# High matmuls of a piece first, the second mixer's projection as 512-column matmuls with folds, its tanh one slot later

## What is computed

```python
h = x
for i in range(2):
    u = rmsnorm(h, norm_mix_g[i])
    h = h + (rglru_mixer if i == 0 else ssd_mixer)(u, ...)
    h = h + swiglu(rmsnorm(h, norm_ffn_g[i]), w_gate[i], w_up[i], w_down[i])
    h = h + sigmoid(rmsnorm(h, norm_ple_g[i]) @ ple_w_gate[i]) * (p[i] @ ple_w_proj[i])
return rmsnorm(h, final_norm_g)

def ssd_mixer(u, ...):
    z, xbc, dt = split(u @ w_in)                  # 4096, 6144 and 64 columns
    xbc = silu(causal_dwconv(xbc, conv_w, conv_b))    # four taps
    xs, B, C = split(xbc)                         # 64 heads of 64; 8 groups of 128 states
    y = ssd_scan(xs, softplus(dt + dt_bias), -exp(a_log), B, C) + d_skip * xs
    y = y * silu(z)
    y = group_rmsnorm(y) * norm_g                 # 8 groups of 512
    return y @ w_out
```

## Time and profile before

| | us |
|---|---|
| median of three runs | 2766.11 |
| the three runs | 2753.71, 2766.11, 2769.26 |
| the profiled execution | 2769.57 |
| its span, first to last instruction | 2767.8 |
| mean granted TensorE clock | 0.993 |
| PE busy | 2708.5 |
| DVE busy | 2031.0 |
| ACT busy | 1342.2 |
| POOL busy | 382.6 |

### The profile page before, as it was taken

How to read it: one execution, slowest core, us unless ns; L and a number is a source line. 1 busy time by engine, 2 the same in 40 slices (tenths; PEclk the granted TensorE clock), 3 DMA queues, 4 the chain that set the end, 5 groups by cost and what they waited for, 6 DMA issues and landing times.

```text
span 2767.8 us, 51496 instructions
## 1 busy us (share of the span) xinstructions
PE 2708.5 (98%) x17871; PEld 2464.4 (89%) x17871; DVE 2031.0 (73%) x2802; ACT 1342.2 (48%) x1818; POOL 382.6 (14%) x418
## 2 busy tenths in 40 slices
PE   7999999999999999999999999999999999999997
PEld 7998888888888888999998999988888888888897
DVE  8887876665666677888886788878666556666776
ACT  5665344444444444456664566634444444444443
POOL 3333200000000121201110011121000000001122
PEclk9999999999999999999999999999999999999999
DMA  5555566656656665555555655556555666565554
GB/s 194 185 180 157 177 197 189 190 175 191 203 190 189 191 191 163 188 169 178 173 178 167 198 172 173 179 157 197 182 186 179 178 201 185 187 187 171 184 178 149
DMA packets 158369, 502.35 MB, mean 181 GB/s; under 512 B 17792, under 2 KB 20160, under 8 KB 157120
## 3 DMA queue, kind: packets, MB, share of 16 engines
q1 hardware_dynamic: 158192, 501.04, 58.1%
q10 hardware_dynamic: 80, 0.07, 0.0%
HBM read 498.88 MB, written 2.16 MB: 181 GB/s over the span
## 4 chain that ended last, share of the span: by engine, by line
PE 83%; DVE 9%; issue 4%; ACT 3%; POOL 1%; DMA 0%; DVEq 0%; ACTq 0%; SPq 0%; POOLq 0%
PE bank L381 42%; PE bank L383 21%; PE bank L364 6%; PE bank L366 6%; PE bank L365 6%; DVE wlo L821 3%; DVE arena L973 2%; ACT whi L575 1%; DVE R L878 0%; DVE arena L975 0%; PE bank L540 0%; DVE arena L1201 0%; PE bank L544 0%; ACT arena L755 0%; PE bank L542 0%
## 5 line engine op out<-in xcount | busy, mean ns | idle before, releaser
L381 PE MATMUL bank<-R,whi 128*128 128x512 f32 x4992 | 1754.5, 397 | 12.0 <-POOL R L1323 6.1
L821 DVE TENSOR_TENSOR wlo<-wraw,whi 128x1024 fp32r<-128x1024 f32 (+3 forms) x1056 | 1208.4, 1155 | 575.6 <-ACT whi L575 572.7
L575 ACT ACTIVATE whi<-wraw 128x1024 fp32r<-128x1024 f32 (+3 forms) x1056 | 993.2, 947 | 955.8 <-PE bank L383 767.1
L383 PE MATMUL bank<-R,wlo 128*128 128x256 f32 x4992 | 1395.2, 279 | 0.0
L381 PEld LDWEIGHTS bank<-R,whi 128*128 128x128 f32 x4992 | 939.5, 188 | 240.3 <-POOL R L1323 8.4
L383 PEld LDWEIGHTS bank<-R,wlo 128*128 128x128 f32 x4992 | 943.2, 189 | 0.1
L364 PE MATMUL bank<-R,whi 128*128 128x256 f32 x2368 | 683.6, 289 | 21.6 <-DVE R L878 13.0
L365 PE MATMUL bank<-R,whi 128*128 128x256 f32 x2368 | 673.0, 284 | 0.0
L366 PE MATMUL bank<-R,wlo 128*128 128x256 f32 x2368 | 672.9, 284 | 0.0
L364 PEld LDWEIGHTS bank<-R,whi 128*128 128x128 f32 x2368 | 456.7, 193 | 30.2 <-issue 15.5
L365 PEld LDWEIGHTS bank<-R,whi 128*128 128x128 f32 x2368 | 457.6, 193 | 2.2 <-issue 1.9
(11 more groups left out here) (165 smaller groups left out, 1365.7 us busy)
## 6 DMA issues: line engine op xcount, KB each, us to landing
wraw<-in_F SPq DMA_DIRECT2D x352, 512.0 KB, 3.9
wraw<-in_B SPq DMA_DIRECT2D x224, 512.0 KB, 3.6
wraw<-in_A SPq DMA_DIRECT2D x96, 512.0 KB, 3.8
wraw<-in_F SPq DMA_DIRECT2D x128, 384.0 KB, 3.1
wraw<-in_F SPq DMA_DIRECT2D x128, 320.0 KB, 3.2
wraw<-in_PL SPq DMA_DIRECT2D x64, 320.0 KB, 3.2
wraw<-in_PL SPq DMA_DIRECT2D x64, 256.0 KB, 2.8
arena<-cs_rows SPq DMA_DIRECT2D x8, 1024.0 KB, 5.8
```

The lines of the kernel that those rows point to most:

```text
L381: nc.tensor.matmul(dst.rearrange("p (s t) -> p s t", s=2), whi[:, q % RING, cols], src[:, :, k, :], start=first, stop=False)
L383: mm = nc.tensor.matmul(dst[:, 0:SEQ], wlo[:, q % RING, cols], src[:, 0, k, :], start=False, stop=last)
L575: nc.scalar.activation(whi[:, slot, 0:w * BLOCK], wraw[:, slot, 0:w * BLOCK], ACT.Copy).then_inc(w_hi, 1)
L821: V.tensor_tensor(wlo[:, slot, 0:w * BLOCK], wraw[:, slot, 0:w * BLOCK], whi[:, slot, 0:w * BLOCK].bitcast(F32), ALU.subtract).then_inc(w_ ...
```

## The change

1. `piece` waits for the high half of the weights, issues the high matmuls of all blocks of the piece, then waits for the low half and issues the low matmuls of all blocks. This holds for every stage, with two high matmuls per block in the narrow ones.
2. B1 joins `WIDE`: its high product becomes one matmul of 512 columns. DVE evacuates with `fold` and a multiply in SBUF.
3. In B1 the tanh of tile nt on ACT and its silu on DVE move from the odd step 2 nt + 3 to the even step 2 nt + 4, behind the taps of the next tile; for the sixth tile they stay at step 13, and the silu goes ahead of the wait for PE.

```diff
--- before.py
+++ after.py
@@ -48,7 +48,7 @@
 LAST_HEAD = {0: (0, 1, 2), 1: (3, 4), 2: (5, 6), 3: (7,)}
 
 
-WIDE = ("A2", "F1", "F2", "B2")
+WIDE = ("A2", "F1", "F2", "B1", "B2")
 GELU_C = 0.7978845608028654
 GELU_S = 0.044715 ** 0.5
 
@@ -368,18 +368,20 @@
             def piece(ph, it, q, blocks):
 
                 p = it * len(ph["widths"]) + ph["piece0"] + q
-                pe.wait_ge(w_lo, p + 1)
+                pe.wait_ge(w_hi, p + 1)
                 for b, (before, dst, src, k, first, last) in enumerate(blocks):
                     for s, v in before:
                         pe.wait_ge(s, v)
                     cols = slice(b * BLOCK, (b + 1) * BLOCK)
-                    if ph["name"] not in WIDE:
-                        mm = three(dst[:, 0:SEQ], whi[:, q % RING, cols], wlo[:, q % RING, cols], src[:, 0, k, :],
-                                   src[:, 1, k, :], first, last)
-                        continue
-
-                    nc.tensor.matmul(dst.rearrange("p (s t) -> p s t", s=2), whi[:, q % RING, cols], src[:, :, k, :],
-                                     start=first, stop=False)
+                    if ph["name"] in WIDE:
+                        nc.tensor.matmul(dst.rearrange("p (s t) -> p s t", s=2), whi[:, q % RING, cols], src[:, :, k, :],
+                                         start=first, stop=False)
+                    else:
+                        nc.tensor.matmul(dst[:, 0:SEQ], whi[:, q % RING, cols], src[:, 0, k, :], start=first, stop=False)
+                        nc.tensor.matmul(dst[:, 0:SEQ], whi[:, q % RING, cols], src[:, 1, k, :], start=False, stop=False)
+                pe.wait_ge(w_lo, p + 1)
+                for b, (before, dst, src, k, first, last) in enumerate(blocks):
+                    cols = slice(b * BLOCK, (b + 1) * BLOCK)
                     mm = nc.tensor.matmul(dst[:, 0:SEQ], wlo[:, q % RING, cols], src[:, 0, k, :], start=False, stop=last)
                 mm.then_inc(w_used, 1)
 
@@ -743,10 +745,6 @@
                                 group_rinv(group - 1)
                             if q == 8 and not first:
                                 group_hi(group - 1, it - 1)
-                            if q % 2 == 1 and 3 <= q <= 13:
-                                nt = q // 2 - 1
-                                act.wait_ge(conv_done, group * 6 + nt + 1)
-                                nc.scalar.activation(cth[:, nt % 2, :], ca[:, nt, :], ACT.Tanh).then_inc(conv_t, 1)
                             if q % 2 == 0 and 2 <= q <= 12:
                                 nt = q // 2 - 1
                                 if nt == 0 and not very_first:
@@ -756,6 +754,10 @@
                                                      bias=flat(bpar[:, at(group), nt * 5 + 4:nt * 5 + 5]),
                                                      scale=flat(bpar[:, at(group), nt * 5 + 3:nt * 5 + 4])
                                                      ).then_inc(tap_done, 1)
+                            if q % 2 == 0 and 4 <= q <= 12 or q == 13:
+                                nt = (q + 1) // 2 - 2
+                                act.wait_ge(conv_done, group * 6 + nt + 1)
+                                nc.scalar.activation(cth[:, nt % 2, :], ca[:, nt, :], ACT.Tanh).then_inc(conv_t, 1)
                             if q == 2 and not first:
                                 y_square(group - 1)
                             if q in (14, 16, 18):
@@ -1125,22 +1127,25 @@
                                 later_taps(cpad[:, nt % 2], ca[:, nt, :],
                                            lambda k, nt=nt, group=group: flat(bpar[:, at(group), nt * 5 + k:nt * 5 + k + 1]),
                                            conv_done)
-                            if q % 2 == 1:
-                                dve.wait_ge(w_used, p + 1)
-                                src = bank[BANKS2[q // 2 % 2]][:, 0:SEQ]
-                            if q % 2 == 1 and q < 12:
-                                nt = q // 2
-                                V.tensor_tensor(cpad[:, nt % 2, 3:3 + SEQ], src, rinv[:], ALU.mult).then_inc(bank_free, 1)
-                            if q % 2 == 1 and 3 <= q <= 13:
-                                nt = q // 2 - 1
+                            if q % 2 == 0 and 4 <= q <= 12 or q == 13:
+                                nt = (q + 1) // 2 - 2
                                 dve.wait_ge(conv_t, group * 6 + nt + 1)
                                 V.scalar_tensor_tensor(out=ca[:, nt, :], in0=cth[:, nt % 2, :], scalar=1.0,
                                                        in1=ca[:, nt, :], op0=ALU.add, op1=ALU.mult).then_inc(silu_done, 1)
+                            if q % 2 == 1:
+                                dve.wait_ge(w_used, p + 1)
+                                src = BANKS2[q // 2 % 2]
+                            if q % 2 == 1 and q < 12:
+                                nt = q // 2
+                                row = cpad[:, nt % 2, 3:3 + SEQ]
+                                fold(src, row)
+                                V.tensor_tensor(row, row, rinv[:], ALU.mult).then_inc(bank_free, 1)
                             if q % 2 == 1 and q > 12:
                                 j = q // 2 - 6
                                 if j == 0 and not very_first:
                                     dve.wait_ge(yn_lo, group * 4)
-                                V.tensor_tensor(zt[:, j, :], src, rinvh[:], ALU.mult).then_inc(bank_free, 1)
+                                fold(src, zt[:, j, :])
+                                V.tensor_tensor(zt[:, j, :], zt[:, j, :], rinvh[:], ALU.mult).then_inc(bank_free, 1)
                             if q in (14, 16, 18):
                                 z_silu(group, q // 2 - 7)
                             if q == 14:
@@ -1201,7 +1206,7 @@
                         V.scalar_tensor_tensor(out=zt[:, j, :], in0=zt[:, j, :], scalar=flat(bpar[:, at(group), 34 + j:35 + j]),
                                                in1=grms[:], op0=ALU.mult, op1=ALU.mult).then_inc(yn_done, 1)
 
-                steps(dve, ph, body, own, {"A1": 18, "B1": 21, "F1": 6, "PL": 0}.get(name, 4))
+                steps(dve, ph, body, own, {"A1": 18, "B1": 31, "F1": 6, "PL": 0}.get(name, 4))
                 own.close()
             dve.wait_ge(h_done, 2 * KT)
             V.tensor_tensor(swi_u[:, 0, :], h[:, KT - 1, :], h[:, KT - 1, :], ALU.mult).then_inc(last_square, 1)
```

## The result

The changed kernel takes 2782.23 us (median of five runs, 2781.48 to 2783.18). The kernel before, run beside it, takes 2766.11 (five runs, 2753.71 to 2771.18). The ratio is 1.0074, 95% interval 1.004 to 1.0108: slower by 0.7%. The forecast was 2758. All five runs of the changed kernel lie within 1.7 us, those of the kernel before within 17.5. The profiled execution took 2781.48 us, with a span of 2779.7 and a mean granted clock of 0.988.

The account below looks back on a forecast made before the run. PE, busy 98% of the span, was taken as the bound, so time is its issue intervals plus few gaps. 2769.6 - 15.3 (rate) - 4.8 (low-half waits) + 5.1 (operand waits) + 3.4 (B1) = 2758 us; range 2732 to 2786.

Parts of the forecast that it names:

- (a): Wide stages, high first: 226.7 + 120 = 346.7 ns a block, no alternation left for the long rhythm; -15.3 us.
- long rhythm: Wide stages: slower rate of alternating matmuls, 353.2 against 346.5 ns a block, costing 15.3 us; rival that it stays, 2773, chance 0.15.
- (c): A1, A2, B2: after a late operand of the last block, eight low matmuls are still to come; +5.1 us.
- fixed cost of 13.3 ns per matmul: Wide and narrow matmuls: one fixed cost each, whatever the order, explains both forms and gives 346.7 ns a block.
- a 512 costs its 0.231 behind another too: Rival, wide stages: 351 ns a block, +7.2 us instead of -15.3, total 2781; chance 0.14.
- The rival in which the weight loads vanish: Wide stages: loads hidden behind 512 columns, 333 ns a block, 81 us less instead of 15.3, total 2692; chance 0.10.
- (d): B1 in wide form: PE 17.0 us less, DVE 7.2 us more a group; B1 in all +3.4 us.
- (e): B1, tanh one slot later: clears the ring in which ACT waited for DVE's taps and DVE for the next whi.
- 46.9 - 4.0: B1, DVE's path to the sixth silu: 46.9 us less 4.0 idle, plus seven folds, gives 47.9 to 48.2 us.
- B1 not bound by DVE: Rival, B1: folds hide in the waits for PE, groups of 62.3 us, total 2732; chance 0.12.
- (b): PL and B1's start: waiting for low halves after the high matmuls wins -4.8 us, clock effects included.
- Clearly slower: Whole kernel: slower than 2779.9 us; chance 0.15.

Follow-up runs that it names:

- the mixture in pairs: The changed kernel with high-first order in batches of two blocks (two high matmuls, then two low); 2772.47 us in one run.
- the late product: The changed kernel with POOL's 1024-wide product in B1 waiting for the sixth silu instead of the second; 2769.66 us, ratio 1.0031.
- The last experiment: Narrow B1, old order in wide stages, high first in B1 and PL, late tanh and product, plus PL's gate bank emptied before the low half; 2754.54 us, ratio 0.9945.
- old order with late product: Kernel before with narrow B1, high first only in B1 and PL, tanh one slot later, POOL's product after the sixth silu; 2752.69 us, ratio 0.9963.

## Why the prediction was wrong, point by point

The profiled execution took 2781.5 us where the sum was 2758. Four terms account for 23 of these 23.5 us. The largest, and the one that turned a gain into a loss, is the rate of the wide form: -15.3 us were set down for it, and about -1 came.

**(a) The rate of the wide form: the mechanism right in part, the term mis-sized.** The step "227 + 120 = 346.7 ns a block everywhere" failed. The long rhythm did go, and one rate took the place of two. But it is 349.2 to 350.3, as each row of wide matmuls starts with intervals of 228 to 236 behind the narrow ones. The wide stages, A2 and B2 among them, changed by +0.5 us (table) where -15.3 for the rhythm and +4.3 for the operand waits had been set down, -11.0 together: 11.5 us off. The rate is more than that. The 4992 wide blocks x 2.7 ns (349.4 on average less 346.7) are 13.5 us, and by the stages the rate gave -0.8 instead of -15.3, 14.5 us off: +6.5 and -7.4 in F1 and F2, -1.2 in A2 (256 blocks, 353.8 to 349.1 ns), +1.3 in B2 (512 blocks, 346.6 to 349.1). The operand waits of A2 and B2 gave 3.0 of it back, see (c).

The reasoning from a fixed cost of 13.3 ns per matmul fitted the two forms of before by coincidence: the earlier trace rows had the alternation 231 and 115, and the mixture in pairs shows 233 and 114 to 119. The rival "a 512 costs its 0.231 behind another too" (2781) is nearest in time, and its even point of 348 ns was passed. Its clear loss was to begin at 351, and 349 to 350 is a little below that; so it holds for five of the eight intervals. The rest of the loss came from B1 and the other terms, and the agreement of its number with the result is luck. The rival in which the weight loads vanish is excluded: 230 ns on average, where the rule of the Trainium skill quoted in the prediction ("TensorE: Matmul & The Clock Gate") gives 216. Why the first five intervals of a row are longer stays open.

**(d), (e) B1: engine right, size wrong by 6.4 us.** DVE bounds the wide B1, as forecast; the late product shows it. The path to the sixth silu came to 48.6 (forecast 47.9 to 48.2), and from PE's start behind it to the end of piece 19 took 18.4 (1311.26 to 1329.65), as forecast. But the group is 67.2, and not 66.3. The step "46.9 - 4.0" plus seven folds failed, by 0.7. It took all waits for a whi or a tap off, and 0.37 of them stayed; with the two other idle times of the row (0.18 and 0.56 before, 0.18 and 0.47 now) that is 0.3. The rest is busy time: POOL's product was in the 46.9 already, where it stretched an operation by 1.55 us, and it stretches another by 2.04 now. The other 0.2 are from the silu's end to PE's start (1311.07 to 1311.26). The sum left this step out; it took 0.14 before (1364.89 to 1365.03). The wait was also not where it was expected. PE did not wait for the silu; it waited 2.8 us from start to start at piece 12, and the clock fell behind that. This used up what PE had to spare, but lengthened the group by under 0.1 us.

The last group of a half is shorter on the same path, 1396.92 to 1444.65, 47.7 us. Its taps show where:

```profile
1396.92 0.69 DVE L965 TENSOR_REDUCE arena<-bank 128x256 f32<-128x512 f32 x1 [0.47 <-PE bank L385]
...
1406.73 1.00 DVE L975 SCALAR_TENSOR_TENSOR arena<-arena,bpar 128x256 f32<-128x256 f32 x2
1407.77 1.41 DVE L977 SCALAR_TENSOR_TENSOR arena<-arena,bpar 128x256 f32<-128x256 f32 x1
...
1444.23 0.42 DVE L1133 SCALAR_TENSOR_TENSOR arena<-arena 128x256 f32<-128x256 f32 x1
```

From the first tap to the last are 1.04 us, where the groups before take 1.25 (1272.21 to 1273.46, above). Over six tiles the difference is 1.3 us, of which 0.4 go again elsewhere on the path. What makes the taps closer is not shown; the kernel before has it too. The steady groups cost 4 x 1.34 + 2 x 1.1 = 7.6 us (forecast 3.9), the first group of half 0 +3.8 (forecast +1.6; 1.1 of it by the order and 2.7 by the wide form, each measured alone), that of half 1 -1.7 (forecast -2.1): +9.8 against +3.4. The rival "B1 not bound by DVE" (2732) is excluded.

**(b) PL and the start of B1: PL right, B1's start wrong in its cause, 3.1 us.** The two PL stages, which contain the gap at B1's start, changed by -1.9 and +0.2; forecast -4.8, 3.1 more. The waits inside PL gave what was forecast: the two stalls of layer 0 went from 1.39 + 2.42 us, start to start, to 0.85 + 1.75, which is 1.2. The step "then 8 x 0.12 = 0.96 remain instead of 2.88, so 1.9 is won" failed. The profile puts the wait at B1's start down to a low half, "6.6, 3, 3.3". DVE, and then PE, in the kernel before:

```profile
1174.18 1.76 DVE L821 TENSOR_TENSOR wlo<-wraw,whi 128x1024 fp32r<-128x1024 f32 x1
1176.88 2.46 DVE L821 TENSOR_TENSOR wlo<-wraw,whi 128x1024 fp32r<-128x1024 f32 x2 [0.94 <-ACT whi L575]
1179.26 0.42 DVE L1092 TENSOR_TENSOR arena<-bank,rinvh 128x256 f32<-128x256 f32 x1
```

```profile
1179.78 0.36 PE L364 MATMUL bank<-R,whi 128*128 128x256 f32 x1 [3.35 <-DVE wlo L821]
```

The low half of B1's first piece is the one of 1174.18. It was done at 1175.94, before PE issued its last matmul of PL (1176.15), so PE did not wait for it at all. The two of 1176.88 are for B1's second and third piece; they stand ahead of L1092 in DVE's list, and the bank that L1092 frees at 1179.68 is what PE waited for. So moving the wait for the low half moved nothing there: the gap is 3.46 instead of 3.62, and the clock stood at its lower level for 6.8 us instead of 3.4. The last experiment moved the bank and won the gap.

**(c) Waits for operands: A1 short by 2.2 us, A2 and B2 over-charged by 3.0.** A1 lost 3.0 instead of 0.8. Its first 50 us, columns as in rows 5:

```profile
10.00:60.00 50.00, 43.42 (x261) 39.31 (x262) 42.94 (x70) 24.92 (x38) 18.84 (x20) 0.90 0.50 178
24.00:34.00 10.00, 9.56 (x63) 9.06 (x64) 7.94 (x12) 2.34 (x2) 1.29 (x2) 0.83 0.41 118
48.00:58.00 10.00, 8.48 (x49) 8.51 (x49) 8.21 (x24) 4.63 (x8) 1.19 (x1) 0.66 0.69 248
```

The granted clock is 0.90 from 10 to 60 us, where it was 0.97 in the kernel before (0.83 and 0.66 in the two ten-microsecond stretches, before 1.00 and 0.83). Two more stretches of 3.4 us at 1.2 GHz cost 1.7 us each. But only a part of this belongs to the order. The four other profiles whose A1 is that of the kernel before have a fall of the clock at 22 us too, and their A1 takes 224.6 to 225.4 us; the six with high first over whole pieces have 225.8 to 226.7. The means are 1.8 us apart, and the 223.4 of the kernel before is the lowest of its five. So about 1 us of the 2.2 is the order, and the rest lies in which execution was profiled. B2's 2.7 are no confirmation of the 2.8 set down for its waits, since 1.3 of them are the rate: its waits cost 1.4. A2 lost nothing by its wait (-1.3 in all, -1.2 of it the rate), where +1.5 was set down.

Sum: 11.5 + 6.4 + 3.1 + 2.2 = 23.2 of 23.5.

**(e) The tanh.** It was worth 0.6 us a group with a narrow B1, and 0.4 in the wide one.

**The chances.** Clearly slower had 0.15. Reading the spread of the kernel before as the rhythm being present or absent fits all runs: beside the experiments they lie in two clusters some 13 us apart (two runs of 54 are some 13 higher again, 2781.3 and 2784.0), and the kernels that run high first everywhere never show two. The long rhythm in one layer's F1 and F2, 2112 blocks x 6.7 ns = 14 us, would give that distance. The median that the ratio is taken against is thus a mean over rhythms. Against 2755 the change costs 27 us, against 2769 some 13.

**What stays open.** What starts the long rhythm. Five profiles have kernels with the alternation, and by their pieces it was in A2 and in layer 1's F1 and F2 (the kernel before); in A2, the first B1 and B2 and a part of the second B1 (wide B1, old order); in A2 alone (the tanh alone); in layer 0's F1 and F2 (old order with late product); and there and in the second B2 (bank first). The code of these stages is equal but for B1. In F1 and F2 the rate was there from the fourth piece of a layer's first F1 at the latest and held to the layer's end, over 700 us and more. In A2 and B2 it was there from the start or changed behind a fall of the clock, as at 261 us in the last two. No experiment made it come or go other than by giving up the alternation. That its share explains each single run was not shown; only the profiled executions were looked into.

## What to carry to other kernels

Measure the rate of a sequence of matmuls in the very order that is planned; the mean cost of two forms doesn't split into costs of single instructions that hold in another order. Before a wait is moved, look up when the very piece of data that it is for was ready. The profile named DVE's low halves here, but the one that PE needed had been made 3.8 us before the wait ended. The list of the engine that released PE (two later low halves, then the bank) beats the name that the profile gives to the wait. Where an engine is to get more work on a path that it bounds, first look for its own operations that another engine stretches: moving one wait on POOL gave back 12.6 us here.

## What was not expected of the hardware

- Alternating 512- and 256-column matmuls have two steady rates, 346.6 and 353.2 ns a pair at full granted clock, from one code and in one execution. In F1 the longer one has mean intervals of 236 and 117 ns for every pair; the shorter one has 231 and 112.5, then 232.5 and 117.5, in turns. Which one is entered changes from run to run. In rows of eight the pair takes 349.2 and in pairs 348.3, each without a second rate in the runs made (for the pairs, one).
- Behind 256-column matmuls, a 512 takes 228 to 236 ns for the first five and 227 from the sixth on.
- A POOL product of 1024 columns held a DVE operation of 256 columns for 2.52 us instead of 0.48.
